# Two activation tables move by 192 bytes in a four-layer diffusion backbone

## The reference, cut to what matters

```
for i in range(4):
    h = x * (1 + scale) + shift                       # per channel, from c (latent) or c_ctx (context)
    y = mixer_i(h_lat, h_ctx)                         # 0 GQA, 1 differential, 2 gated linear, 3 neighbourhood
    x = layer_norm(alpha * x + gate * y)
    h = x * (1 + scale) + shift
    u = dwconv3(h @ w_up)                             # w_up 1024 x 5632
    f = (silu(u[:, :2816]) * u[:, 2816:]) @ w_down    # w_down 2816 x 1024
    x = layer_norm(alpha * x + gate * f)
return x_lat                                          # in the last layer, after the mixer, the latents alone
```

## The kernel before

| table | byte before | modulo 128 | byte after | modulo 128 |
|---|---|---|---|---|
| h_hi | 17,536 | 0 | 17,728 | 64 |
| h_lo | 33,920 | 0 | 34,112 | 64 |
| slab_raw, slab_hi, slab_lo (4,096 apart) | 50,304 to 95,360 | 0 | 50,816 to 95,872 | 0 |
| cst | 99,456 | 0 | 99,968 | 0 |
| g_first_hi | 109,504 | 64 | 109,632 | 64 |
| g_first_lo | 104,192 | 0 | 105,536 | 64 |
| summed | 178,368 | 64 | same | 64 |
| g_hi, g_lo | 129,216, 174,272 | 64 | same | 64 |
| z_hi, z_lo | 202,688, 204,736 | 64 | same | 64 |

## Time and profile before

### The profile page before, as it was taken

How to read it: one execution, slowest core, us unless ns; L and a number is a source line. 1 busy time by engine, 2 the same in 40 slices (tenths; PEclk the granted TensorE clock), 3 DMA queues, 4 the chain that set the end, 5 groups by cost and what they waited for, 6 DMA issues and landing times.

```text
span 2413.2 us, 35782 instructions
## 1 busy us (share of the span) xinstructions
PE 2340.2 (97%) x13872; PEld 1903.1 (79%) x13872; DVE 1696.3 (70%) x2583; ACT 1129.2 (47%) x1948; POOL 335.6 (14%) x269
## 2 busy tenths in 40 slices
PE   6999999999999989999999999899999999989998
PEld 3765888888888559888879877788888889848998
DVE  3376689988444777999875236768999845487875
ACT  3466643442442576434324444455434325386663
POOL 0000311111110003111112003422111102002110
PEclk9999999999999999999999999999999999999999
DMA  8621645557233113555563421043555645404664
GB/s 260 204 71 39 215 142 164 166 148 208 81 97 92 30 58 100 166 157 166 162 180 86 113 70 45 2 132 114 166 163 158 192 116 125 129 13 123 187 180 132
DMA packets 449420, 310.94 MB, mean 129 GB/s; under 512 B 11922, under 2 KB 404674, under 8 KB 448996
## 3 DMA queue, kind: packets, MB, share of 16 engines
q1 hardware_dynamic: 446480, 307.09, 43.2%
q10 hardware_dynamic: 2772, 1.56, 0.2%
HBM read 307.56 MB, written 1.05 MB: 128 GB/s over the span
## 4 chain that ended last, share of the span: by engine, by line
PE 85%; DVE 6%; ACT 4%; issue 2%; DMA 2%; ACTq 0%; SPq 0%; DVEq 0%
PE bank L1690 74%; PE bank L1973 2%; DMA slab_raw<-in_mod_w 2%; PE bank L1993 1%; PE bank L2037 1%; ACT p L793 1%; DVE slab_lo L1047 1%; DVE stat L1316 1%; ACT hb L610 1%; DVE q_part L1375 1%; PE bank L1749 1%; PE bank L1768 1%; ACT slab_hi L595 1%; ACT pt L805 1%; PE bank L2165 1%
## 5 line engine op out<-in xcount | busy, mean ns | idle before, releaser
L1690 PE MATMUL bank<-h_hi,slab_hi 128*128 128x512 f32 (+1 forms) x2416 | 841.9, 348 | 4.1 <-DVE h_lo L1112 2.5
L1690 PE MATMUL bank<-h_hi,slab_lo 128*128 128x512 f32 (+1 forms) x2416 | 828.9, 343 | 0.0
L1690 PE MATMUL bank<-h_lo,slab_hi 128*128 128x512 f32 (+1 forms) x2416 | 828.9, 343 | 0.0
L1047 DVE TENSOR_TENSOR slab_lo<-slab_raw,slab_hi 128x1024 fp32r<-128x1024 f32 (+1 forms) x388 | 526.2, 1357 | 296.1 <-ACT slab_hi L595 294.8
L595 ACT ACTIVATE slab_hi<-slab_raw 128x1024 fp32r<-128x1024 f32 (+1 forms) x388 | 400.8, 1034 | 303.8 <-PE bank L1690 228.0
L1690 PEld LDWEIGHTS bank<-h_hi,slab_hi 128*128 128x128 f32 x2416 | 458.0, 190 | 85.6 <-issue 19.8
L1690 PEld LDWEIGHTS bank<-h_hi,slab_lo 128*128 128x128 f32 x2416 | 458.0, 190 | 53.8
L1690 PEld LDWEIGHTS bank<-h_lo,slab_hi 128*128 128x128 f32 x2416 | 458.3, 190 | 53.3 <-issue 0.5
L1021 ACT ACTIVATE conv<-bank,prm 128x512 f32<-128x512 f32 (+1 forms) x176 | 127.7, 725 | 446.6 <-PE bank L1690 446.6
L1072 DVE SCALAR_TENSOR_TENSOR mod_sum<-slab_raw,cond_wide,mod_sum 128x512 f32<-128x512 f32 x420 | 316.5, 812 | 0.3 <-DMA slab_raw<-in_mod_w 0.2
L1690 PE MATMUL bank<-g_hi,slab_hi 128*128 128x512 f32 (+1 forms) x788 | 272.0, 345 | 0.0
(11 more groups left out here) (248 smaller groups left out, 2658.0 us busy)
## 6 DMA issues: line engine op xcount, KB each, us to landing
slab_raw<-in_ffn_w_up SPq DMA_DIRECT2D x176, 512.0 KB, 3.9
slab_raw<-in_mod_w SPq DMA_DIRECT2D x168, 512.0 KB, 4.6
slab_raw<-in_ffn_w_down SPq DMA_DIRECT2D x64, 512.0 KB, 3.6
slab_gap<-in_mod_w SPq DMA_DIRECT2D x24, 512.0 KB, 7.6
slab_raw<-in_ffn_w_down SPq DMA_DIRECT2D x32, 384.0 KB, 3.2
slab_raw<-in_b_w_qkv SPq DMA_DIRECT2D x24, 512.0 KB, 3.8
slab_raw<-in_c_w_in SPq DMA_DIRECT2D x24, 512.0 KB, 3.8
slab_raw<-in_d_w_qkv SPq DMA_DIRECT2D x24, 512.0 KB, 3.8
```

Of the source, the lines that this page charges most:

```text
L1047: nc.vector.tensor_tensor(wlo[slot][:, 0:w], raw[of][:, 0:w], whi[slot][:, 0:w].bitcast(f32), ALU.subtract).then_inc(s_lo, 1)
L1690: ins = mm(out, l, r, start=first and n == 0, stop=last and n == 2, skip_group_check=parted)
```

## The change

No computation, no instruction and no wait is changed; on every engine the same instructions stand in the same order. Four small tables change their places in the row of `place` calls. `coef0` (192 bytes) now stands ahead of `h_hi`, so `h_hi` and `h_lo` move by 192 bytes. `coef1` (192) and `small` (128) now stand behind `h_lo`, so the weight slots and `cst` move by 512. `modT` and `unit_gb` go ahead of `prm`, which moves by 1,344 bytes, and with it `g_first_lo` and `q_dec1`, which lie in the same place. `mod_row`, `spread`, `g_first_hi`, `w_gate` and `cond_wide` move by 128. From `mean` on nothing moves.

```
         xn = place("xn", [P, DT, T])
+        coef = [place("coef0", [P, 6, DT])]
         h_at = [top[0]]
         h_hi, h_lo = place("h_hi", [P, DT, T], f32r), place("h_lo", [P, DT, T], f32r)
+        coef.append(place("coef1", [P, 6, DT]))
+        small = place("small", [P, 32])
         raw = [place(f"slab_raw{s}", [P, SLAB]) for s in range(SLOTS)]
         whi = [place(f"slab_hi{s}", [P, SLAB], f32r) for s in range(SLOTS)]
         wlo = [place(f"slab_lo{s}", [P, SLAB], f32r) for s in range(SLOTS)]
         cst = place("cst", [P, K_N])
+        modT = [place(f"modT{s}", [P, N_MOD * DT, 2]) for s in range(2)]
+        unit_gb = place("unit_gb", [P, 2, DT])
         prm_at = [top[0]]
         prm = place("prm", [P, DEPTH * R_LAYER])
-        modT = [place(f"modT{s}", [P, N_MOD * DT, 2]) for s in range(2)]
-        coef = [place(f"coef{s}", [P, 6, DT]) for s in range(2)]
-        unit_gb = place("unit_gb", [P, 2, DT])
...
-        small = place("small", [P, 32])
         mean_at = [top[0]]
```

## The result

The changed kernel takes 2421.59 us (median of four runs, 2421.15 to 2426.03), the kernel before 2410.8 us beside it. The ratio is 1.0042 with an interval of 1.003 to 1.0054: slower by 0.42%, some 10 us, where "no change that can be told" was the forecast. The time lies inside the predicted range of 2398 to 2426 us, outside the forecast's own of 2406 to 2417.

A forecast was written before the change was run, and what follows sets the result against it. PE was taken as the bound; 512-column losses and 256-column gains, with small terms, summed to +1.8 us: 2411.4 us on the median of 2409.6. Predicted range 2398 to 2426 us, the forecast's own 2406 to 2417.

The forecast's parts named there:

- The bound: Whole kernel: PE bounds it, busy 2340.2 of 2413.2 us, with 74% of the wait chain on one matmul line.
- what counts is whether the stream and the block being loaded stand alike modulo 128: All matmul streams: alike gives 226.7 and 120.0 ns; unlike about 229 for 512 columns, 113 to 118 for 256.
- I take `g`, since its blocks have 128 columns: `h` past weights, 512 columns: `g`'s 228.9 ns taken as the new distance, +2.2 ns each, instead of `z`'s +5.8.
- first rival: Up, projections, value weights: 512-column streams cost 232.5 ns as with `z`, +27.0 us; sum +18.5, 2428 us; chance 20%.
- 512 columns of h: `h` streaming past weights, 4,080 matmuls of 512 columns: +2.2 ns each, +9.0 us.
- 512 weight columns past h: Weights streaming past `h` blocks, 576 matmuls of 512 columns: the same +2.2 ns each, +1.3 us.
- 256 columns of h: `h` past weights, 3,168 matmuls: -2.2 ns each, -7.0 us; 384 behind a 512-column stream a further -4.4 ns, -1.7 us.
- The choice of 117.8: `h`'s 256-column streams: most take 117.8 ns, not 113.4, since they start behind a wait or another 256-column stream.
- second rival: 256-column streams of `h` settle at 113.4 ns, -20.9 us; sum -10.8, 2399 us; chance 20%, including a smaller 512-column loss.
- Masks, z, 256 weight columns: Masks past gate blocks in `h` +0.5 us; `h` past `z` -0.1; layer 0's 96 matmuls of 256 weight columns -0.2.
- `down` unchanged: `g` past weights in `down`: distances stay at 228.9, 113.4 and 117.8 ns, no change.
- constant within each: Matmul timelines before the change: start distances constant within each stretch, which a chance collision with DVE, ACT or DMA would not be.

The follow-up runs named there:

- h at +64: Against the kernel before, `h` moved by 64 bytes and the weights by 256, stream minus block +64 modulo 256: 2413.06 us, ratio 1.0001.
- both by 192: Changed kernel with `coef1` and `small` behind the weight slots, so `h` and slots both move by 192 bytes: 2419.29 us, ratio 1.0029 to the kernel before.
- h at +128: Against the kernel before, `h` moved by 128 bytes and the weights by 512, stream minus block 128 modulo 256: 2436.38 us, ratio 1.0098.

## Why the prediction was right in its range and wrong in its mechanism

- **The bound: right.** PE is 97% busy, no wait grew by more than 0.8 us, and a sum over distances of PE's matmuls alone gives the measured change. `down` kept its 512-column distance.
- **The step that failed: "what counts is whether the stream and the block being loaded stand alike modulo 128."** What counts is the signed difference modulo 256: four cases, of which the rows before held 0 (`h`), +64 (`g`) and, in 24 matmuls, -64 (`h` past `z`). The change makes `h` past weights -64. From it followed "I take `g`, since its blocks have 128 columns": `g` is at +64. The row that stood at the right difference was `z`'s 232.5 ns; the first rival had even noted the sign. Run "h at +64" shows the two cases side by side, and "both by 192" and "h at +128" show that alike modulo 128 is not enough.
- **512 columns of h:** +9.0 us taken, +25.5 measured. The first rival had the mechanism and the price (5.8 ns; 6.2 measured).
- **512 weight columns past h:** +1.3 taken, +0.8 measured. Here the first rival would have been wrong: this pair is at +64, and 229.1 ns is `g`'s distance.
- **256 columns of h:** -7.0 and -1.7 taken, -17.3 measured. The choice of 117.8 for what "starts behind a wait or another 256-column stream" failed both ways: behind its wait, layer 3's up ran at 113.3 ns, and `g`'s context halves, straight behind a 512-column stream, at 117.7. This was the second rival's price (-20.9), reached to four fifths.
- **Masks, z, 256 weight columns:** +0.5, -0.1, -0.2 taken; +0.2, -0.1, -0.2 measured.
- **`down` unchanged:** false for the context halves, +1.2 us.
- **Two readings of the rows:** "constant within each" is not so for `g` past weights with 512 columns, where the trace has the cycle of 226, 229 and 232 ns. And eight distances read at 0.01 us can't tell 118.8 from 117.8 ns, so the masks were too coarse a row to be evidence.

Two terms were too small, by 16.5 and 8.6 us, with opposite signs, and the difference is most of the 8 us by which the sum missed. The two rivals were not rivals: both came true at once, each for its own shape. The prediction weighed them as alternatives, and so its chances had no case for their sum, +27.0 - 20.9 and some. That the time fell into the range is luck: the range had been drawn wide enough for either rival alone, and the two misses took most of each other away.

The page "SBUF — State Buffer" of the Trainium skill, section "Who interferes with whom", gives TensorE two read ports, one for the moving operand and one for the weight load, and calls them independent. The runs do not agree that the two never meet: with nothing but the place of tables changed, the same matmuls take 226.7 to 233.3 ns and 113.3 to 120.0 ns, by the difference of the two operands' addresses. Where in the chip they meet, no run shows.

## What to carry to other kernels

Where TensorE is the bound and streams of one shape run back to back, list for each pair the address of the stream less that of the block loaded behind it, modulo 256, and read the distance between starts for each value. In this kernel 0 is best for 512 columns and -64 or +64 for 256; 128 costs 512 columns nearly as much as -64 (232.7 ns) and wins 256 columns 1.3 ns at most. All of this is shown for fp32r alone. A layout that looks alike in all tables can be wrong for one stage, and tables can be placed by stage. When a trace holds two likenesses for a term, ask in which respect each is like, sign included, before choosing by shape.

## What the runs showed that was not expected

- Distance between starts of fp32r matmuls with 128x128 blocks, granted clock 1.00, by d modulo 256: 0, 226.7 ns (512 columns) and 120.0 (256); +64, 229.0 and 113.3 or 117.7; 128, about 232.7 and 118.6 to 120.0; -64, 233.3 and 113.3 or 117.7.
- Half a stream is not half the time: at -64 two of 256 columns take 226.6 ns, one of 512 takes 233.3.
- A stretch holds 113.3 or 117.7 ns to its end, the same in another execution. Moving tables that neither operand of the stretch shares changed which, and in every record it went with the last distance ahead of the stretch.
- 64 columns of `z` as the block fit the same rule at -64 (232.8 ns) and at +64 (228.9, in "h at +128"); at 128 they took 229.3 and 229.7 ns and at 0 229.8. 24 matmuls are too few to say why.
